# Where the modulation products of a two-layer trunk are computed: layer 1's moved into layer 0's out projection, the gate's into the attention groups

## The chip, the cores and the metric

The kernel runs on one core of a Trainium2 chip. The metric is the device time in microseconds, the median of several executions. A core has TensorE (PE in the profile; its weight loads are the row PEld), VectorE (DVE), ScalarE (ACT), GpSimd (POOL) and SyncE (SP, which here only starts DMAs). They run their own instruction streams and wait for each other on semaphores.

## The reference

Two layers over 512 tokens of width 2048, batch 1, in float32. Each layer computes, with the vector c that is the same for both layers:

```
mod = silu(c) @ w_mod[l] + b_mod[l]          # 2048 -> 3 * 2048
shift, scale, gate = split(mod, 3)
h = x * (1 + scale) + shift
p = h @ w_in[l]                              # all projections
y_nsa = nsa(...)         * silu(nz)          # 6 heads, 2 groups of 3
y_gdn = gated_delta(...) * silu(gz)          # 6 heads
y_sb  = stick_breaking(...) * silu(sz)       # 4 heads
y = concat(y_nsa, y_gdn, y_sb) @ w_out[l]    # 2048 -> 2048
x = layernorm(alpha * x + (1 + gate) * y, ln_g[l], ln_b[l])
```

`shift` and `scale` of a layer are needed at its very start, `gate` only in its out projection. `mod` depends on nothing but c and the weights, so it can be computed at any earlier time.

## The kernel before

**Matrix products.** Each float32 weight is split into a high and a low part, and a product is three TensorE passes (high x high, low x high, high x low; L439 to L441 in `column_tile`, L810 to L812 in the out projection). Weights are streamed as halves of 128 x 1024 numbers (512 KB) through a ring of four SBUF slots (`ring`, `NS = 4`). SP loads them strictly in the order of the stream (L383), each into the slot of the item four places before it, once that slot is free (`raw_free0` to `raw_free3`). GpSimd splits a half in two instructions, `w_hi` (L1170) and `w_lo` (L1172), into one of two buffers, and then frees the slot. It has to wait until TensorE has used the buffer (`split_used`). A column tile is two halves, 48 matmuls.

**Modulation products.** For layer 0, shift and scale are computed at the start of the kernel. All others go through the same ring, as items "M" between the weight items "C" and the compression weights "D": a half row block of `w_mod` (128 x 1024), which VectorE multiplies by 128 numbers of silu(c) and adds to `acc` (`add_mod`, one SCALAR_TENSOR_TENSOR on VectorE, which then frees the slot). 32 of these make one part of `mod` (2048 numbers, still to be summed over 128 partitions). Before them VectorE fills `acc` with zeros (a MEMSET of 128 x 2048) and ScalarE loads a row of `b_mod` into it (`start_sums`, L846). Behind them TensorE sums over the partitions: for shift and scale `reduce_mod` (L455, 16 matmuls with one column, two instructions each, and a copy to `modT`), for the gate four pairs of matmuls against ones (L785).

**Stages of a layer.** (1) h is built and transposed, with a small product. (2) Two attention groups (a hardware loop), each with 14 column tiles: eight first, then three heads of 11 steps, two tiles a head spread over the steps. In a head each step has scores on TensorE, a maximum on VectorE, an exponential on ScalarE, a normalisation on VectorE, transposes and the product with the values. `MOD_STEPS` says at which steps VectorE takes which Ms, ahead of its own work in that step. VectorE's last instruction of a head writes `yT`. (3) Six GDN heads. (4) Four stick-breaking heads, the first two in a loop with four column tiles each, then one with two tiles and one with one. (5) The out projection: four blocks of 512 columns, each of 8 halves (24 matmuls each) in eight banks used in turn; when a block is done, VectorE adds x, with three instructions for each of four token tiles, while TensorE is at the next block. (6) The norm, whose statistics VectorE has gathered.

**Where the Ms stand before.** Layer 0's groups take layer 1's shift (group 0) and scale (group 1): 32 Ms a group, two behind each C of the first and second head, four behind each C of the third; VectorE takes one at each of steps 0 to 7 (two in the third head). A group ends with the reduction on TensorE and a copy on VectorE. The gate's 32 Ms stand in the stick-breaking heads of each layer, eight a head. Layer 1's groups have none.

**Order.** Everything is written out by hand: the lists of items in the functions below give the order of the stream, and GpSimd's and VectorE's programs and SP's loads are derived from them. SP and GpSimd use hardware loops for the groups and lots; SP also has a loop over four slots.

Of the kernel before, what the change touches and what calls it, by code (L numbers as in the profile page):

```python
# [18 lines left out]
P = 128  # L19
# [23 lines left out]
NS = 4  # L43
# [39 lines left out]
SB_3_ITEMS = mixed(range(1), 0) + [("M", m) for m in range(8)]  # L83
GROUP_TILES = 14
LAYER_TILES = KVH * GROUP_TILES + (N_LOTS - 1) * LOT
OUT_HALVES = 2 * KT
LEVELS = (2, 4, 8, 16, 32)


def layout(has_next):  # L90

    group = len(group_items(has_next))
    at, n = {"group": SMALL_HALVES, "group_len": group}, SMALL_HALVES + KVH * group
    at["first"] = n
    n += len(FIRST_TILE)
    at["gdn"] = n
    n += GDN_H * len(GDN_ITEMS)
    at["sb"] = n
    n += (SB_H - 2) * len(SB_ITEMS)
    at["sb_2"] = n  # L100
    n += len(SB_2_ITEMS)
    at["sb_3"] = n
    n += len(SB_3_ITEMS)
    at["out"] = n
    at["end"] = n + OUT_HALVES
    return at


LAYOUTS = [layout(l < DEPTH - 1) for l in range(DEPTH)]
STREAM_AT = [sum(a["end"] - SMALL_HALVES for a in LAYOUTS[:l]) for l in range(DEPTH)]  # L110
# [54 lines left out]
def build(nc, x, positions, c, b_mod, mod0, small_cols, stream, small, lns, const, out, where, layers=DEPTH):  # L165
    x_norm = nc.dram_tensor("x_norm", (TT, P, DM), F32, kind="Internal").ap()
    ctx = ExitStack()
    with ctx:
# [55 lines left out]
        ln_gb = yT[:, 4:12, :].rearrange("p (a b) c -> p a (b c)", a=2)  # L224
        acc0 = [acc[:, :], arena[:, 16:20, :].rearrange("p a b -> p (a b)")]
# [72 lines left out]
        def spread(n, weights):  # L298
# [18 lines left out]
        MOD_STEPS = [{s: (s, s + 1) for s in range(8)}, {s: (8 + s, 9 + s) for s in range(8)},  # L317
                     {s: (16 + 2 * s, 18 + 2 * s) for s in range(8)}]
# [31 lines left out]
        turn_of_out = [(HALVES_AT[l] + LAYOUTS[l]["out"]) // NS for l in range(DEPTH)]  # L350
        sums_before = [2 + l + 2 * min(l, DEPTH - 1) for l in range(DEPTH)]
# [3 lines left out]
        def _(sp):  # L355
# [12 lines left out]
            for l in range(layers):  # L368
# [9 lines left out]
                def load(first, n):  # L378

                    with sp.Fori(0, n // NS) as n4:  # L380
                        for i in range(NS):
                            sp.wait_ge(S(f"raw_free{i}"), n4 + ((HALVES_AT[l] + first) // NS + 1))
                            sp.dma_start(ring[:, i, :], stream[bass.ds(  # L383
                                n4 * NS + (STREAM_AT[l] + first - SMALL_HALVES + i), 1)].rearrange(
                                    "a p n -> (a p) n")).then_inc(S(f"slot_in{i}"), 16)

                at = LAYOUTS[l]
                load(SMALL_HALVES, at["out"] - SMALL_HALVES)
                if l < layers - 1:

                    sp.wait_ge(S("y_ready"), after("y_ready", l * 16 + NSA_H + GDN_H))
                    sp.dma_start(sm_all[:, :], small[l + 1]).then_inc(S("small_in"), 16)
                load(at["out"], OUT_HALVES)
# [11 lines left out]
        def _(pe):  # L405
# [45 lines left out]
            def reduce_mod(sums, n):  # L451

                pe.wait_ge(S("mod_sum"), n)
                for k in range(KT):
                    last = mm(MB[:, k:k + 1], sums[:, k * P:(k + 1) * P], ones[:, 0:1], start=True, stop=True)  # L455
# [6 lines left out]
            for l in range(layers):  # L462
# [7 lines left out]
                for k in range(KT + 3):  # L470
                    if k < KT:
                        if k >= 4:

                            pe.wait_ge(S(("h_even", "h_odd")[k % 2]), l * (KT // 2) + k // 2 - 1)
                        for t in range(TT):
# [28 lines left out]
                with pe.Fori(0, KVH) as g:  # L504
# [117 lines left out]
                    if l < DEPTH - 1:  # L622

                        reduce_mod(acc, g + (sums_before[l] + 1))

# [93 lines left out]
                if l < DEPTH - 1:  # L719
                    pe.wait_ge(S("mod_copied"), 2 * l + 4)  # L720
# [68 lines left out]
                pe.wait_ge(S("mod_sum"), sums_before[l] + (3 if l < DEPTH - 1 else 1))  # L789
                gate(0, 2)  # L790
                for n in range(TT):
                    outs = (bank[2:6], ODD)[n % 2]
                    for k2 in range(KT // 2):
# [21 lines left out]
                        last.then_inc(S("split_used"), 1)  # L815


        @block.scalar
        def _(act):
# [34 lines left out]
            for l in range(layers):  # L854
# [36 lines left out]

                with act.Fori(0, KVH) as g:
# [869 lines left out]
```

## Time and profile before

| | us |
|---|---|
| median of 3 runs | 3161.83 |
| lowest and highest | 3160.68, 3165.58 |
| span of the profiled execution | 3166.5 |
| TensorE busy (86% of the span) | 2713.5 |
| VectorE busy (51%) | 1605.2 |
| GpSimd busy (47%) | 1502.6 |
| ScalarE busy (24%) | 746.3 |

The times of the runs are not split by execution, so of the profiled one only its span is given, from the first instruction to the last. A share of busy time is an average over stages that have different limits. To see what a stage is worth, the timeline shows where it begins and ends, and the views of waits and windows show who stands still in it and for whom. Matmuls overlap in the records, so the pitch from one start to the next says more than a matmul's duration.

### The profile page before, as it was taken

To read this page: it belongs to the slowest core of one execution; us is meant where nothing else is said; L and a number is where in the kernel's file an instruction comes from. 1 tells how busy PE (TensorE), PEld (TensorE's weight loads), DVE (VectorE), ACT (ScalarE), POOL (GpSimd) and SP (SyncE) were. 2 spreads that over 40 slices of the span, in tenths; PEclk is the share of its full clock that TensorE was granted. 3 is DMA by queue.
4 is the path that set the end of the run, shared out by engine and by line. 5 is a ranking of instruction groups with operands and counts; after the bars stand their busy time and mean duration, and the time that the engine had idled before them with its cause. 6 is when DMAs were issued, how large, how long until landed. Compare 5 with 4: busy or idle time off the path is not lost.

```text
span 3166.5 us, 39541 instructions
## 1 busy us (share of the span) xinstructions
PE 2713.5 (86%) x13072; PEld 2152.6 (68%) x13072; DVE 1605.2 (51%) x1975; ACT 746.3 (24%) x1332; POOL 1502.6 (47%) x692
## 2 busy tenths in 40 slices
PE   0598789878888899988987999998988888998995
PEld 0476577667777777765866777776767777775674
DVE  8615732767555553565234143146556555356535
ACT  0201100213333332333002021023323233334100
POOL 7254336433333434554762744734333334464675
PEclk9999989989999999998998999999999999998997
DMA  9433442441111111344324213211111111234431
GB/s 351 188 120 113 160 134 87 150 142 47 47 46 46 46 40 54 131 158 159 95 74 140 87 54 100 87 54 54 47 46 41 45 46 47 94 133 153 156 124 73
DMA packets 82843, 314.28 MB, mean 99 GB/s; under 512 B 9974, under 2 KB 10230, under 8 KB 76822
## 3 DMA queue, kind: packets, MB, share of 16 engines
q1 hardware_dynamic: 76608, 295.78, 28.8%
q10 hardware_dynamic: 6108, 16.83, 1.5%
q8 instruction: 78, 1.28, 0.2%
q14 instruction: 49, 0.40, 0.0%
HBM read 304.18 MB, written 8.39 MB: 99 GB/s over the span
## 4 chain that ended last, share of the span: by engine, by line
PE 44%; DVE 25%; POOLq 12%; issue 9%; ACT 4%; DMA 2%; DVEq 2%; ACTq 2%; SPq 0%
DVE arena L1216 16%; PE bank L439 8%; PE bank L441 8%; PE bank L440 8%; POOLq L1173 6%; DVE acc L1216 5%; POOLq L1171 5%; PE bank L418 3%; ACT L822 2%; PE bank L810 2%; PE bank L812 2%; PE bank L811 2%; ACT arena L822 2%; PE bank L412 2%; DVE tiny L1216 2%
## 5 line engine op out<-in xcount | busy, mean ns | idle before, releaser
L1170 POOL TENSOR_TENSOR w_hi<-ring,cst 128x1024 fp32r<-128x1024 f32 (+1 forms) x328 | 626.2, 1909 | 1575.6 <-PE bank L441 1065.4
L439 PE MATMUL bank<-h_hi,w_hi 128*128 128x512 f32 x2048 | 904.0, 441 | 46.1 <-POOLq L1173 42.9
L1172 POOL TENSOR_TENSOR w_lo<-ring,w_hi 128x1024 fp32r<-128x1024 f32 (+1 forms) x328 | 809.8, 2469 | 47.9 <-issue 0.4
L441 PE MATMUL bank<-h_hi,w_lo 128*128 128x512 f32 x2048 | 830.9, 406 | 0.0
L440 PE MATMUL bank<-h_lo,w_hi 128*128 128x512 f32 x2048 | 828.6, 405 | 0.0
L439 PEld LDWEIGHTS bank<-h_hi,w_hi 128*128 128x128 f32 x2048 | 404.5, 198 | 142.1 <-POOLq L1173 45.8
L441 PEld LDWEIGHTS bank<-h_hi,w_lo 128*128 128x128 f32 x2048 | 401.7, 196 | 92.4
L440 PEld LDWEIGHTS bank<-h_lo,w_hi 128*128 128x128 f32 x2048 | 404.9, 198 | 80.0 <-issue 13.2
L822 ACT ACTIVATE arena<-bank 128x512 f32<-128x512 f32 (+5 forms) x316 | 155.0, 490 | 982.2 <-PE bank L441 399.7
L1216 DVE SCALAR_TENSOR_TENSOR acc<-ring,cact,acc 128x1024 f32<-128x1024 f32 x128 | 216.9, 1694 | 46.0 <-DMA ring<-in_stream 29.7
L810 PE MATMUL bank<-w_hi,h_hi 128*128 128x512 f32 x512 | 202.8, 396 | 7.5 <-POOLq L1173 7.5
L822 ACT ACT_TABLE_LOAD x147 | 188.6, 1283 | 74.8 <-issue 64.8
L812 PE MATMUL bank<-w_hi,h_lo 128*128 128x512 f32 x512 | 200.6, 392 | 0.0
L811 PE MATMUL bank<-w_lo,h_hi 128*128 128x512 f32 x512 | 200.3, 391 | 0.0
L418 PEld LDWEIGHTS bank<-arena 128*128 128x128 f32 x864 | 133.9, 227 | 95.3 <-issue 87.1
L418 PE MATMUL bank<-arena 128*128 128x64 f32 x864 | 132.1, 305 | 75.0 <-DVEq L1501 49.9
L1216 DVE TENSOR_TENSOR arena<-arena,cst 128x512 f32<-128x512 f32 (+2 forms) x160 | 141.5, 885 | 38.1 <-ACT arena L822 24.0
L1216 DVE SCALAR_TENSOR_TENSOR state<-state,arena,bank 128x128 f32<-128x128 f32 x96 | 33.3, 347 | 243.8 <-PE bank L708 242.3
L1216 DVE SCALAR_TENSOR_TENSOR arena<-raw,conv_h,arena 128x512 f32<-128x512 f32 x108 | 143.6, 1329 | 9.8 <-issue 1.1
L822 ACT ACTIVATE arena<-bank,tiny 128x512 f32<-128x512 f32 (+3 forms) x132 | 75.5, 572 | 307.7 <-DVE tiny L1216 306.6
L822 ACT ACTIVATE arena<-arena 128x512 f32<-128x512 f32 (+5 forms) x186 | 95.8, 515 | 219.9 <-DVE arena L1216 187.2
L1216 DVE TENSOR_TENSOR arena<-arena,bank 128x512 f32<-128x512 f32 (+3 forms) x140 | 77.1, 551 | 131.3 <-PE bank L418 88.2
(183 smaller groups left out, 3158.0 us busy)
## 6 DMA issues: line engine op xcount, KB each, us to landing
ring<-in_stream SPq DMA_DIRECT2D x480, 512.0 KB, 3.7
yT<-in_mod SPq DMA_DIRECT2D x32, 1024.0 KB, 6.1
arena<-in_x SPq DMA_DIRECT2D x1, 4096.0 KB, 15.4
arena<-in_x ACTq DMA_DIRECT2D x4, 1024.0 KB, 10.9
x_norm<-arena ACTq DMA_DIRECT2D x4, 1024.0 KB, 7.0
arena<-x_norm ACTq DMA_DIRECT2D x4, 1024.0 KB, 9.1
out<-arena SPq DMA_DIRECT2D x4, 1024.0 KB, 3.9
raw<-in_lns ACTq DMA_DIRECT2D x8, 256.0 KB, 5.9
```

Source lines behind the costliest of these rows:

```text
L418: last = mm(narrow(dst)[:, t, :], lhs[:, t * P:(t + 1) * P], narrow(rhs)[:, t, :], start=True, stop=True)
L439: mm(PJ[b][:, :], hi, h_hi[:, k, :], start=(k == 0), stop=False)
L440: mm(PJ[b][:, :], hi, h_lo[:, k, :], start=False, stop=False)
L441: last = mm(PJ[b][:, :], lo, h_hi[:, k, :], start=False, stop=(k == KT - 1))
L810: mm(outs[t][:, :], h_hi[:, k, at], hi, start=(k == 0), stop=False)
L811: mm(outs[t][:, :], h_hi[:, k, at], lo, start=False, stop=False)
L812: last = mm(outs[t][:, :], h_lo[:, k, at], hi, start=False, stop=(k == KT - 1))
L822: made = act.activation(*args, **kw)
L1170: pool.tensor_tensor(w_hi[:, par, 0:w], ring[:, slot, 0:w], one.broadcast_to((P, w)), ALU.mult)
L1172: pool.tensor_tensor(w_lo[:, par, 0:w], ring[:, slot, 0:w], w_hi[:, par, 0:w].bitcast(F32), ALU.subtract)
L1173: pool.drain().then_inc(S("split_ready"), 1)
L1216: made = op(*args, **kw)
```

## The change

The Ms of layer 1's shift and scale leave layer 0's two attention groups and go into layer 0's out projection (64 of them), into two accumulators in `yT` (`next_acc`, blocks 4 to 11, free by then). `NEXT_MODS` gives how many Ms stand behind each half: none behind the first two or three halves of a block, three behind each of the last five (two at the very end). VectorE takes all Ms of a block before it adds x for that block. Both reductions follow TensorE's last matmul of the stage, in banks 2 and 3, and VectorE copies them before the norm. The gate's Ms leave stick-breaking and go into the groups of both layers, 16 a group: one behind each C in the first and third head, two in the second; VectorE takes them at steps 1, 4, 6 and 8. So both layers' groups are now alike, and the gate needs one fill and one row of `b_mod` ahead of the groups. The stream lies in memory as before; SP's loads, GpSimd's splits of the out projection and their addresses are written out in the new order.

```diff
+ORDER_GROUP = (mixed((0, 1), 0) + [("D", i) for i in range(8)] + mixed(range(2, 8), 0) + mixed((8, 9), 1)
+               + mixed((10, 11), 2, 4) + mixed((12, 13), 1, 12))
+ORDER_LOT, ORDER_LOT_2, ORDER_LOT_3 = (mixed(range(i), 0) for i in (LOT, 2, 1))
+NEXT_MODS = ((0, 0, 0, 3, 3, 3, 3, 3), (0, 0, 2, 3, 3, 3, 3, 3), (0, 0, 1, 3, 3, 3, 3, 3), (0, 0, 2, 3, 3, 3, 3, 2))
+def order_out(has_next):
+    items, m = [], 0
+    for n in range(TT):
+        for k2 in range(KT // 2):
+            items.append(("C", n, k2))
+            for _ in range(NEXT_MODS[n][k2] if has_next else 0):
+                items.append(("M", m))
+                m += 1
+    return items
...
+        next_acc = [yT[:, 4 * i:4 * i + 4, :].rearrange("p a b -> p (a b)") for i in (1, 2)]
...
-        MOD_STEPS = [{s: (s, s + 1) for s in range(8)}, {s: (8 + s, 9 + s) for s in range(8)},
-                     {s: (16 + 2 * s, 18 + 2 * s) for s in range(8)}]
+        MOD_STEPS = [{1: (0, 1), 4: (1, 2), 6: (2, 3), 8: (3, 4)}, {1: (4, 6), 4: (6, 8), 6: (8, 10), 8: (10, 12)},
+                     {1: (12, 13), 4: (13, 14), 6: (14, 15), 8: (15, 16)}]
...
 SP:
+                    slot, turn = (HALVES_AT[l] + p) % NS, (HALVES_AT[l] + p) // NS
+                    sp.wait_ge(S(f"raw_free{slot}"), turn + 1)
+                    sp.dma_start(ring[:, slot, :], stream[STREAM[key]]).then_inc(S(f"slot_in{slot}"), 16)
...
 TensorE, after a group (removed) and after the out projection (added):
-                    if l < DEPTH - 1:
-                        reduce_mod(acc, g + (sums_before[l] + 1))
...
+                if l < DEPTH - 1:
+                    pe.wait_ge(S("o_used"), after("o_used", l * 16 + 12))
+                    for part in range(2):
+                        reduce_mod(next_acc[part], gate_sum[l] + 1 + part, bank[2 + part])
...
 ScalarE, before its loads of x:
                 act.wait_ge(S("y_split"), l * 16 + MIX_T)
+                if l < DEPTH - 1:
+                    for part in range(2):
+                        start_sums(gate_sum[l] + 1 + part, next_acc[part][0:1, :], l + 1, part)
...
 VectorE, in the out projection:
+                if has_next:
+                    for part in range(2):
+                        fill(next_acc[part], 0.0).then_inc(S("acc_zero"), 1)
+                    dve.wait_ge(S("bmod_in"), (gate_sum[l] + 2) * 16)
                 for n in range(TT):
+                    if has_next:
+                        for m in range(sum(map(sum, NEXT_MODS[:n])), sum(map(sum, NEXT_MODS[:n + 1]))):
+                            add_mod(m, ORDER_OUT[l], l, "out", sums=next_acc[m // (2 * KT)])
+                            if m % (2 * KT) == 2 * KT - 1:
+                                sync().then_inc(S("mod_sum"), 1)
...
+                if has_next:
+                    for part in range(2):
+                        dve.wait_ge(S("mod_done"), 2 * l + 3 + part)
+                        cp(modT[:, part, :], bank[2 + part][:, 0:KT]).then_inc(S("mod_copied"), 1)
                 dve.wait_ge(S("rstd_ready"), l + 1)
```

## Rows read from the trace of the kernel before

**Rows 1.** The page: busy time; a group of instructions (busy, mean ns of one | idle before).

```profile
PE 2713.5 (86%) x13072; PEld 2152.6 (68%) x13072; DVE 1605.2 (51%) x1975; ACT 746.3 (24%) x1332; POOL 1502.6 (47%) x692
L1216 DVE SCALAR_TENSOR_TENSOR acc<-ring,cact,acc 128x1024 f32<-128x1024 f32 x128 | 216.9, 1694 | 46.0 <-DMA ring<-in_stream 29.7
```

**Rows 2.** Windows: from:to us, busy us of each engine, granted clock, DMA share, GB/s.

```profile
1350.00:1354.00 4.00, 4.00 (x10) 3.13 (x11) 3.42 (x3) 0.31 (x1) 3.85 (x2) 0.50 0.72 246
1476.00:1652.00 176.00, 171.43 (x753) 140.92 (x751) 48.70 (x54) 1.92 (x2) 132.08 (x64) 1.00 0.34 109
1862.00:1901.00 39.00, 37.66 (x197) 29.54 (x196) 19.73 (x48) 10.56 (x28) 17.43 (x9) 1.00 0.19 55
```

**Rows 3.** Timeline, start and duration in us: layer 0's out projection, first and last matmul.

```profile
1471.00 0.79 PE L810 MATMUL bank<-w_hi,h_hi 128*128 128x512 f32 x1
...
1647.04 0.39 PE L812 MATMUL bank<-w_hi,h_lo 128*128 128x512 f32 x1
```

**Rows 4.** Timeline, VectorE: starts and ends of attention heads, start of GDN, both layers.

```profile
268.72 1.28 DVE L1216 SCALAR_TENSOR_TENSOR acc<-ring,cact,acc 128x1024 f32<-128x1024 f32 x1 [0.30 <-issue]
...
314.90 0.69 DVE L1216 SCALAR_TENSOR_TENSOR yT<-bank,arena 128x512 f32 x1 [0.21 <-issue]
...
360.87 0.69 DVE L1216 SCALAR_TENSOR_TENSOR yT<-bank,arena 128x512 f32 x1 [0.21 <-issue]
...
420.30 0.69 DVE L1216 SCALAR_TENSOR_TENSOR yT<-bank,arena 128x512 f32 x1 [5.68 <-PE bank L618]
...
729.96 0.17 DVE L1216 MEMSET state<- 128x128 f32 x1 [0.29 <-issue]
...
1822.43 0.29 DVE L1216 SCALAR_TENSOR_TENSOR arena<-bank,cst 128x124 f32<-128x124 f32 x1 [0.38 <-PE bank L579]
...
1861.96 0.69 DVE L1216 SCALAR_TENSOR_TENSOR yT<-bank,arena 128x512 f32 x1 [0.22 <-issue]
...
1900.95 0.69 DVE L1216 SCALAR_TENSOR_TENSOR yT<-bank,arena 128x512 f32 x1 [0.22 <-issue]
...
1937.72 0.69 DVE L1216 SCALAR_TENSOR_TENSOR yT<-bank,arena 128x512 f32 x1 [4.53 <-PE bank L618]
...
2202.80 0.17 DVE L1216 MEMSET state<- 128x128 f32 x1 [0.30 <-issue]
```

**Rows 5.** Waits in stick-breaking, layer 0: us in total, times, longest.

```profile
PE bank L439 <- POOLq L1173: 11.0, 3, 4.6
```

**Rows 6.** Timeline: a reduction; steps 1 and 6 of a layer 1 head; a fill.

```profile
698.43 6.10 PE L455 MATMUL bank<-cst,acc 128*128 128x1 f32 x32 [1.00 <-DVEq L1400]
...
1866.80 0.29 DVE L1216 TENSOR_REDUCE tiny<-bank 128x1 f32<-128x128 f32 x1 [0.56 <-PE bank L590]
...
1883.83 0.42 DVE L1216 TENSOR_REDUCE tiny<-bank 128x1 f32<-128x256 f32 x1 [1.64 <-PE bank L590]
...
2177.02 1.76 DVE L1216 MEMSET acc<- 128x2048 f32 x1 [0.71 <-issue]
```

**Rows 7.** Timeline, VectorE and GpSimd: an M beside splits.

```profile
1404.19 2.35 POOL L1172 TENSOR_TENSOR w_lo<-ring,w_hi 128x1024 fp32r<-128x1024 f32 x1
1404.29 3.33 DVE L1216 SCALAR_TENSOR_TENSOR acc<-ring,cact,acc 128x1024 f32<-128x1024 f32 x1
...
1406.86 2.51 POOL L1170 TENSOR_TENSOR w_hi<-ring,cst 128x1024 fp32r<-128x1024 f32 x1 [0.32 <-issue]
```

**Rows 8.** Timeline, GpSimd and SP, and DMA issues (KB, us to landing): layer 0's out projection.

```profile
1573.40 2.39 POOL L1172 TENSOR_TENSOR w_lo<-ring,w_hi 128x1024 fp32r<-128x1024 f32 x1
1576.08 0.33 SPq L383 DMA_DIRECT2D ring<-in_stream  x1
1576.80 1.90 POOL L1170 TENSOR_TENSOR w_hi<-ring,cst 128x1024 fp32r<-128x1024 f32 x1 [1.01 <-PE bank L812]
...
ring<-in_stream SPq DMA_DIRECT2D x28, 512.0 KB, 3.6
```

**Rows 9.** Timeline, VectorE: the norm's first operation.

```profile
1655.99 0.16 DVE L1216 SCALAR_TENSOR_TENSOR tiny<-meanvar,tiny 128x4 f32<-128x4 f32 x1 [1.99 <-ACT tiny L822]
```

More of the change, by code:

```diff
@@ L86, with layout @@
 OUT_HALVES = 2 * KT
+ORDER_OUT = [order_out(l < DEPTH - 1) for l in range(DEPTH)]
 LEVELS = (2, 4, 8, 16, 32)
-def layout(has_next):
-    group = len(group_items(has_next))
+def layout(l):
+    group = len(ORDER_GROUP)
     at, n = {"group": SMALL_HALVES, "group_len": group}, SMALL_HALVES + KVH * group
     at["first"] = n
-    n += len(FIRST_TILE)
+    n += len(ORDER_LOT_3)
     at["gdn"] = n
-    n += GDN_H * len(GDN_ITEMS)
+    n += GDN_H * len(ORDER_LOT)
     at["sb"] = n
-    n += (SB_H - 2) * len(SB_ITEMS)
+    n += (SB_H - 2) * len(ORDER_LOT)
     at["sb_2"] = n
-    n += len(SB_2_ITEMS)
+    n += len(ORDER_LOT_2)
     at["sb_3"] = n
-    n += len(SB_3_ITEMS)
+    n += len(ORDER_LOT_3)
     at["out"] = n
-    at["end"] = n + OUT_HALVES
+    at["end"] = n + len(ORDER_OUT[l])
     return at
-LAYOUTS = [layout(l < DEPTH - 1) for l in range(DEPTH)]
-STREAM_AT = [sum(a["end"] - SMALL_HALVES for a in LAYOUTS[:l]) for l in range(DEPTH)]
+LAYOUTS = [layout(l) for l in range(DEPTH)]
+STREAM = stream_index()
 HALVES_AT = [sum(a["end"] for a in LAYOUTS[:l]) for l in range(DEPTH)]
@@ L348, in place @@
             return at % NS, at // NS + more
-        turn_of_out = [(HALVES_AT[l] + LAYOUTS[l]["out"]) // NS for l in range(DEPTH)]
-        sums_before = [2 + l + 2 * min(l, DEPTH - 1) for l in range(DEPTH)]
+        gate_sum = [2 + 3 * l + 1 for l in range(DEPTH)]
         @block.sync
@@ L376, in _ @@
                     sp.dma_start(ring[:, i, 0:4 * N_SMALL], small_cols[l, i]).then_inc(S(f"slot_in{i}"), 16)
[L378 to L393, printed above, removed]
+                for i, key in enumerate(order(l)):
+                    p = SMALL_HALVES + i
+                    if p == LAYOUTS[l]["out"] and l < layers - 1:
+                        sp.wait_ge(S("y_ready"), after("y_ready", l * 16 + NSA_H + GDN_H))
+                        sp.dma_start(sm_all[:, :], small[l + 1]).then_inc(S("small_in"), 16)
+                    slot, turn = (HALVES_AT[l] + p) % NS, (HALVES_AT[l] + p) // NS
+                    sp.wait_ge(S(f"raw_free{slot}"), turn + 1)
+                    sp.dma_start(ring[:, slot, :], stream[STREAM[key]]).then_inc(S(f"slot_in{slot}"), 16)
             for t in (1, 0, 2, 3):
@@ L1555, in split_y, with stick @@
                     tt(h_lo[:, k, :], yT[:, k, :], h_hi[:, k, :].bitcast(F32), Su).then_inc(S("y_split"), 1)
-                def stick(h, kind, items, first_k, more=0):
+                def stick(h, kind):
                     last = kind == "sb_3"
@@ L1575, in stick @@
                     for s in range(TT + 1):
-                        if s < TT:
-                            for m in (2 * s, 2 * s + 1):
-                                add_mod(m, items, l, kind, more, first_k)
-                            if last and s == TT - 1:
-                                dve.sem_inc(S("mod_sum"), 1)
                         if s < TT:
```

91 lines of the change are left out of this document (51 added, 40 removed).

## The prediction

> **What bounds the kernel now.** I read first the page's busy shares: TensorE 86%, VectorE 51%, GpSimd 47% [rows 1]. So TensorE is the base, and time is lost or won only where it waits. Then I cut the span into stages with the view of windows. In layer 0's out projection TensorE is busy 171 of 176 us at the full clock, and GpSimd, which splits each weight half into high and low parts, only 132 [rows 2]: TensorE sets the pace there, 32 halves between 1471.0 and 1647.4, 5.44 us each (first and last matmul in [rows 3]; 1.7 us of it is the gate's matmuls). In the attention groups the timeline is the view to read, because both layers run the same code there but for the modulation products (I call one such product, 128x1024, an M): layer 0 has 32 of them in each group, layer 1 none. The heads end at the writes to yT [rows 4]: layer 0's three heads take 46.2, 46.0 and 59.4 us with 8, 8 and 16 Ms, layer 1's 39.5, 39.0 and 36.8. That is the price list of an M in a head. In stick-breaking TensorE waits three times for GpSimd's splits, 11.0 us in a layer [rows 5], since Ms and weights share the four ring slots.
>
> **The change, part by part.** The sum is made against the profiled execution's own span, 3166.5 us; that is 4.7 us (0.15%) above the median of 3161.83, and the difference found is added to the median.
>
> *1. The 64 Ms of layer 1 leave layer 0's groups.* With them go two fills, two b_mod loads and two reductions on TensorE (32 instructions, 6.1 us each [rows 6]). All this together is the difference of the same stretch in both layers [rows 4]: layer 0 from 268.72 to 729.96, 461.2 us, layer 1 from 1822.43 to 2202.80, 380.4 us. Without Ms layer 0 would be like layer 1: **-81 us**. This is the surest term, a few us either way.
>
> *2. 16 gate Ms enter each of the four groups.* 4, 8 and 4 in the three heads, at steps 1, 4, 6 and 8, in pairs in the middle head. VectorE's idle time before its maximum in layer 1 is between 0.56 us (step 1) and 1.64 us (step 6) at these steps [rows 6], so an M of 1.28 us plus 0.1 to its neighbour is covered in part. By the price list: in layer 0's middle head the M of step 0 stands alone in a serial chain (2.5 us from yT to the next operation in place of 0.4: 2.1); the other seven cost 46.0 - 39.0 - 2.1 = 4.9, or 0.7 each. Doubling them, in the third head, adds 22.6 - 7.0 = 15.6 for eight, so 1.95 each, as no idle time is left. New: heads with 4 singles 2.8, the head with four pairs 4 x 0.7 + 4 x 1.95 = 10.6, a group 16 and four groups about **+62 us**. Bounds: +22 if the new places hide all but the second M of each pair (16 of 1.38 us), +108 if nothing is hidden (64 at the mean of 1694 ns [rows 1]).
>
> *3. Fill and b_mod load between groups and GDN go.* Layer 1 shows the fill alone, directly between yT and the convolutions that everything behind waits for [rows 6]: 1.76 + 0.1 us, twice, **-4 us**. The one fill now ahead of the groups stands beside TensorE's first two column tiles (16 halves would be 87 us, 4 are 22): nothing. If that cover were gone it would be 1.9 us in layer 1.
>
> *4. 32 Ms leave stick-breaking in each layer.* TensorE's three waits for splits, 4.6, 4.4 and 2.0 us, go [rows 5]. After the second the granted clock was 0.50 (the level of 1.2 GHz [rows 2]) and twelve matmuls came at 0.43 in place of 0.23 us: 2.4 more, for two heads. In the last head the pair of Ms ends at 1457.0, and the logarithm that the next operation needs was ready about 1455.6 (table load and 0.63): 1.4. Sum 17 per layer, **-34 us**; ends: -22 (the waits alone) and -50 (8 us more a layer, if the pairs of Ms in the third head, 6.2 us at 1404.29, were in the path too).
>
> *5. 64 Ms enter layer 0's out projection.* First the port. An M and a split never run together: in [rows 7] the M that begins inside w_lo (ends 1406.54) ends at 1407.62, 1.08 later, and the w_hi that begins inside the M ends 1.75 after that, at 1409.37. w_lo, 2.39 alone [rows 8], holds on in the same way for about 2.23. So the stage needs 32 x 3.98 + 64 x 1.08 + 16 VectorE sums of about 0.6 = 206 us of one thing, where TensorE needs 174. That alone is +30.
> Then the ring. Behind each of the last five halves of a column block come three Ms, so with four slots the next half falls into the slot of the half before it, and can't be fetched until that one is split. One turn, from [rows 8]: slot free to SP's issue 0.3 (1575.79 to 1576.08), landing 3.6, start 0.1, w_hi's start to w_lo's end 4.4 (1.9, 0.1 and 2.39), and one M of 1.08 between: **9.5 us** against TensorE's 5.44. There are 19 such turns. A block after the first: 8.5 for its first half, about 5.2 for each of three that are prefetched while VectorE drains the block before, 4 x 9.5: 62.3 against 43.5, three times, +56. The first block: its Ms wait for the gate (VectorE's two adds end 1491.1), two fills (3.7) and a b_mod load (2.5 at a guess, since 60 KB took 1.8), and the fifth half stands behind them in SP's queue and beside the 4 MB of x, which ScalarE now issues only after the fills: landed about 1509, split 1515, two more turns, TensorE done at 1541 in place of 1516: +25. Sum **+81 us**. Bounds: +30 (port alone), +123 (19 turns with landing 4.4 and two Ms, 11 us each, and 17 at the start). I take the turn, since every piece of it has a row.
> Here a rule is to be weighed. The Trainium skill (SBUF — State Buffer, Who interferes with whom) says that a VectorE instruction with two SBUF inputs and a GpSimd instruction that reads SBUF exclude each other for the whole instruction, so 64 x 1.28 in place of 64 x 1.08: by the page this stage would need 13 us more of the port. The row has 1.08, so I leave that out. The same page (The DMA setup-cost knee) gives 2 us and the bytes at 436 GB/s, 3.2 us for a half, an estimate; by it the turns would be 8 us cheaper in all. Here too the row, 3.6, is used.
>
> *6. The two reductions at the end of layer 0.* They stand behind the last matmul, 12.2 us (twice the 6.1), and VectorE waits for them before its two copies and the norm: about 12.8 us from the last matmul to the norm's first operation. Before it was 8.6 (1647.4 to 1655.99 [rows 9]), with ScalarE's square root in it, which is now covered: **+4 us**.
>
> *7. SP's and GpSimd's loops written out*: no instruction on the path takes longer for it; SP's issue is 0.33 us of each 5 us. Nothing; +1 to +5 if the longer program is fetched late.
>
> Sum: -81 + 62 - 4 - 34 + 81 + 4 = **+28 us**, so 3161.8 + 28 = **3190 us**.
>
> **The rivals.**
> *A. Only the port binds in the out projection (ends faster).* If halves and Ms are served so that the next half is always in a slot in time, part 5 is +30 and the whole -23: **3139 us**. For it: the loads before landed in 3.6 us, less than a half's time on TensorE. Against: the slot, which nothing but the split frees. It decides from a turn of about 8 us: 19 x 1.5 below mine is the 28 us.
> *B. The new places in the heads hide the Ms.* Part 2 is +22: -12, **3150 us**. For it: VectorE is busy 20 of 39 us in a head of layer 1 [rows 2]. Against: an M a step cost 0.7 there in steps with as much idle time.
> *C. TensorE's clock falls in the out projection.* It waits 4 us in each turn, and after such a wait the clock stood at half for 5 us [rows 2]. At 2.4 us a turn this stays inside the 9.5. If it stays at the low level (1.2 GHz), a half takes 24 x 0.43 = 10.3 us and the stage 330: 73 above the forecast, **3263 us**.
>
> **How the numbers follow.** A difference of 0.2% (6.3 us) is about what a measurement of this kernel can tell. Forecast 0.60 (3165 to 3212; 0.58 slower, 0.02 same). A 0.17 (0.13 faster, 0.04 same), B 0.13 (0.08 and 0.05), C 0.10, slower. Together faster 0.21, same 0.11, slower 0.68. The range, 3148 to 3215, takes in B, the upper part of A and the lower of C.
>
> **What would show it.** Layer 0's stretch between its groups and GDN should be about 410 us and layer 1's also (461 and 380 before); stick-breaking 191 in place of 208; TensorE's stage of the out projection 257 in place of 176, with GpSimd waiting for the ring in 19 turns of about 9.5 us, and w_lo's start to the next w_hi's 5 or more apart; the norm 13 us behind the last matmul. I am wrong if GpSimd finds its slot filled in these turns (A), if heads with four Ms take under 41 us (B), or if the granted clock of the stage is under 0.7 (C).

## The result and the profile after

| | before | changed |
|---|---|---|
| median of 4 runs, us | 3161.26 | 3188.61 |
| lowest and highest | 3159.99, 3165.58 | 3186.42, 3195.72 |
| span of the profiled execution | 3166.5 | 3187.2 |
| mean granted clock | 0.941 | 0.942 |

The ratio is 1.0089, with a 95% interval from 1.0072 to 1.0107: the changed kernel is slower by 0.9%, 27 us, where the prediction had 28 (3190 us). The spans differ by 20.7 us, less than the medians, since the profiled execution of the kernel before was the slowest of its four (3165.58).

The page of the changed kernel (busy us, share of the span; then one group: busy, mean ns of one | idle before). Against [rows 1], TensorE is busy 6.7 us longer for the same number of matmuls, so the other 14 of the 20.7 us are idle time. VectorE is busy 29.5 us longer for the same number of instructions:

```profile
PE 2720.2 (85%) x13072; PEld 2152.8 (68%) x13072; DVE 1634.7 (51%) x1975; ACT 746.2 (23%) x1332; POOL 1511.4 (47%) x692
L1256 DVE SCALAR_TENSOR_TENSOR yT<-ring,cact,yT 128x1024 f32<-128x1024 f32 x64 | 125.7, 1964 | 64.6 <-DMA ring<-in_stream 59.2
```

The timeline of the changed kernel (start, duration): the rows that answer to [rows 3, 4, 9] (heads of group 0 of layer 0, start of GDN, end of GDN and of stick-breaking, first matmul of the out projection, its two reductions, norm; then layer 1's first head and start of GDN).

```profile
268.05 0.29 DVE L1256 SCALAR_TENSOR_TENSOR arena<-bank,cst 128x124 f32<-128x124 f32 x1 [0.39 <-PE bank L625]
309.37 0.69 DVE L1256 SCALAR_TENSOR_TENSOR yT<-bank,arena 128x512 f32 x1 [0.21 <-issue]
360.45 0.69 DVE L1256 SCALAR_TENSOR_TENSOR yT<-bank,arena 128x512 f32 x1 [0.21 <-issue]
402.52 0.69 DVE L1256 SCALAR_TENSOR_TENSOR yT<-bank,arena 128x512 f32 x1 [4.51 <-PE bank L664]
...
683.74 0.17 DVE L1256 MEMSET state<- 128x128 f32 x1 [0.29 <-issue]
...
1219.48 0.75 DVE L1256 SCALAR_TENSOR_TENSOR yT<-arena,sm_all 128x512 f32<-128x512 f32 x1
...
1401.54 1.05 PE L850 MATMUL bank<-w_hi,h_hi 128*128 128x512 f32 x1
...
1406.81 0.69 DVE L1256 SCALAR_TENSOR_TENSOR yT<-bank,arena 128x512 f32<-128x512 f32 x1
...
1655.22 11.05 PE L499 MATMUL bank<-cst,yT 128*128 128x1 f32 x64
...
1662.02 0.17 DVE L1256 COPY modT<-bank 128x16 f32<-128x16 f32 x1 [0.17 <-issue]
1666.31 0.17 DVE L1256 COPY modT<-bank 128x16 f32<-128x16 f32 x1 [4.11 <-PE bank L499]
1666.57 0.16 DVE L1256 SCALAR_TENSOR_TENSOR tiny<-meanvar,tiny 128x4 f32<-128x4 f32 x1
...
1831.57 0.29 DVE L1256 SCALAR_TENSOR_TENSOR arena<-bank,cst 128x124 f32<-128x124 f32 x1 [0.39 <-PE bank L625]
...
2248.52 0.17 DVE L1256 MEMSET state<- 128x128 f32 x1 [0.29 <-issue]
```

Stick-breaking is taken from VectorE's last output of GDN to its last output of the stick-breaking heads. In the kernel before these two rows are:

```profile
1267.78 0.75 DVE L1216 SCALAR_TENSOR_TENSOR yT<-arena,sm_all 128x512 f32<-128x512 f32 x1
...
1476.02 0.69 DVE L1216 SCALAR_TENSOR_TENSOR yT<-bank,arena 128x512 f32<-128x512 f32 x1
```

Subtracting such rows gives the table of stages, in us:

| stretch | before | changed | difference | predicted |
|---|---|---|---|---|
| layer 0, first head to GDN | 461.2 | 415.7 | -45.5 | -51 |
| layer 0, stick-breaking | 208.2 | 187.3 | -20.9 | -17 |
| layer 0, out projection, first to last matmul | 176.4 | 253.8 | +77.4 | +81 |
| layer 0, last matmul to the norm's first operation | 8.6 | 11.2 | +2.6 | +4 |
| layer 1, first head to GDN | 380.4 | 417.0 | +36.6 | +30 |
| layer 1, stick-breaking | 208.5 | 187.0 | -21.5 | -17 |
| layer 1, out projection | 188.4 | 185.1 | -3.3 | 0 |

The waits of the changed kernel in 1402 to 1656 us, layer 0's out projection (engine and what it works on <- whom it waits for: us in total, times, longest), and the same for SP's queue in 1440 to 1650:

```profile
POOL w_hi L1213 <- DMA ring<-in_stream: 89.7, 19, 17.6
DVE yT L1256 <- DMA ring<-in_stream: 59.2, 24, 6.1
PE bank L850 <- POOLq L1216: 53.3, 18, 17.2
```

```profile
SPq L437 <- POOLq L1217: 137.2, 26, 6.6
SPq L437 <- DVE yT L1256: 33.0, 34, 1.7
```

These are the turns of the prediction's part 5 (its parts are called steps from here on), and the reader can go round one: TensorE waits for a split; GpSimd waits for its slot to be filled, 19 times; SP, which would fill it, waits for GpSimd to free that slot. Two turns in the timeline, GpSimd and VectorE (it answers to [rows 8]; w_hi to w_hi 8.15 and 9.59 us):

```profile
1504.76 1.90 POOL L1213 TENSOR_TENSOR w_hi<-ring,cst 128x1024 fp32r<-128x1024 f32 x1 [3.80 <-DMA ring<-in_stream]
1506.81 2.37 POOL L1215 TENSOR_TENSOR w_lo<-ring,w_hi 128x1024 fp32r<-128x1024 f32 x1
1507.15 5.87 DVE L1256 SCALAR_TENSOR_TENSOR yT<-ring,cact,yT 128x1024 f32<-128x1024 f32 x3 [2.35 <-DMA ring<-in_stream]
1512.91 1.90 POOL L1213 TENSOR_TENSOR w_hi<-ring,cst 128x1024 fp32r<-128x1024 f32 x1 [3.73 <-DMA ring<-in_stream]
1514.95 2.34 POOL L1215 TENSOR_TENSOR w_lo<-ring,w_hi 128x1024 fp32r<-128x1024 f32 x1
1515.01 6.11 DVE L1256 SCALAR_TENSOR_TENSOR yT<-ring,cact,yT 128x1024 f32<-128x1024 f32 x3 [2.00 <-DMA ring<-in_stream]
1522.50 1.90 POOL L1213 TENSOR_TENSOR w_hi<-ring,cst 128x1024 fp32r<-128x1024 f32 x1 [5.21 <-DMA ring<-in_stream]
```

The window of the stage, which answers to [rows 2] (busy us of PE, PEld, DVE, ACT, POOL; granted clock; DMA share; GB/s), and the landing of the loads in 1440 to 1650 us:

```profile
1420.00:1662.00 242.00, 188.46 (x742) 148.19 (x741) 168.49 (x120) 1.32 (x2) 133.22 (x60) 0.89 0.62 215
...
ring<-in_stream SPq DMA_DIRECT2D x83, 512.0 KB, 4.8
```

No engine is busy for more than 188 of the 242 us: what limits this stage is a chain that goes through a buffer, not a full engine.

### The profile page after: what moved, and what is told of

It is laid out like the page before. It is cut to its first block, busy times and chain, and to the rows that moved or that the text cites. A ratio compares the mean times of both kernels' runs of the same rounds, so it can differ in the third digit from the quotient of the medians.

```text
span 3187.2 us, 38168 instructions
## 1 busy us (share of the span) xinstructions
PE 2720.2 (85%) x13072; PEld 2152.8 (68%) x13072; DVE 1634.7 (51%) x1975; ACT 746.2 (23%) x1332; POOL 1511.4 (47%) x692
## 3 DMA queue, kind: packets, MB, share of 16 engines
q8 instruction: 78, 1.28, 0.2%
## 4 chain that ended last, share of the span: by engine, by line
PE 51%; DVE 25%; issue 8%; POOLq 7%; ACT 5%; ACTq 2%; DVEq 2%; DMA 1%; SPq 0%
DVE arena L1256 16%; PE bank L483 10%; PE bank L485 9%; PE bank L484 9%; POOLq L1216 4%; DVE acc L1256 4%; POOLq L1214 3%; PE bank L462 3%; ACT L867 2%; PE bank L850 2%; PE bank L852 2%; PE bank L851 2%; ACT arena L867 2%; DVE tiny L1256 2%; PE bank L456 2%
## 5 line engine op out<-in xcount | busy, mean ns | idle before, releaser
L1213 POOL TENSOR_TENSOR w_hi<-ring,cst 128x1024 fp32r<-128x1024 f32 (+1 forms) x328 | 633.8, 1932 | 1586.7 <-PE bank L485 1133.3
L483 PE MATMUL bank<-h_hi,w_hi 128*128 128x512 f32 x2048 | 897.2, 438 | 21.5 <-POOLq L1216 16.6
L850 PE MATMUL bank<-w_hi,h_hi 128*128 128x512 f32 x512 | 212.3, 415 | 59.7 <-POOLq L1216 59.5
L1256 DVE TENSOR_TENSOR arena<-arena,cst 128x512 f32<-128x512 f32 (+2 forms) x160 | 160.5, 1003 | 37.9 <-ACT arena L867 23.8
L850 PEld LDWEIGHTS bank<-w_hi,h_hi 128*128 128x128 f32 x512 | 100.4, 196 | 94.1 <-POOLq L1216 71.7
L1256 DVE SCALAR_TENSOR_TENSOR yT<-ring,cact,yT 128x1024 f32<-128x1024 f32 x64 | 125.7, 1964 | 64.6 <-DMA ring<-in_stream 59.2
```

What stands on the lines that cost most here:

```text
L483: mm(PJ[b][:, :], hi, h_hi[:, k, :], start=(k == 0), stop=False)
L850: mm(outs[t][:, :], h_hi[:, k, at], hi, start=(k == 0), stop=False)
L1213: pool.tensor_tensor(w_hi[:, par, 0:w], ring[:, slot, 0:w], one.broadcast_to((P, w)), ALU.mult)
L1256: made = op(*args, **kw)
```

## Experiments

Each ran on one chip together with the kernel before; ratios are against that kernel, with 95% intervals. The changed kernel stands at 1.0089.

### Slot or port: the out projection taken apart

**The port alone.** Nothing is loaded for the Ms, and VectorE multiplies a fixed tile.

```diff
-            for _ in range(NEXT_MODS[n][k2] if has_next else 0):
+            for _ in range(0):
...
-                            add_mod(m, ORDER_OUT[l], l, "out", sums=next_acc[m // (2 * KT)])
+                            part = next_acc[m // (2 * KT)][:, m % 2 * HALF:(m % 2 + 1) * HALF]
+                            k = m // 2 % KT
+                            stt(part, acc[:, m % 2 * HALF:(m % 2 + 1) * HALF], cact[:, 1, k:k + 1], part, M, Ad)
```

> The changed kernel, but the 64 products of the out projection are multiplied from a fixed SBUF tile and nothing is loaded into the ring for them (layer 1's shift and scale are therefore not what they should be). VectorE and its use of SBUF stay as they are, the ring slots are free for weight halves. If the slot turn sets the pace (my theory: the next half falls into the slot that the last one still holds), the stage falls from 253.8 us to what the shared port alone allows, 32 x 3.98 + 64 x 1.08 + 10 = 206 to 212 us, and the total from 3188.6 to about 3147. If the shared port between VectorE and GpSimd is the cost (rival), the stage stays at about 250 us and the total at about 3188.

Measured: 3159.27 us, ratio 1.0001 (0.9987 to 1.0014). TensorE's stage is 191.9 us, below the 206 to 212 of the slot theory; but the norm begins 43.7 us after its last matmul, in place of 11.2, and so the total misses the expected 3147 by 12 us. The timeline of VectorE in this run shows why:

```profile
1546.32 43.56 DVE L1256 SCALAR_TENSOR_TENSOR yT<-acc,cact,yT 128x1024 f32<-128x1024 f32 x16
...
1590.16 0.39 PE L852 MATMUL bank<-w_hi,h_lo 128*128 128x512 f32 x1
...
1599.80 21.68 DVE L1256 SCALAR_TENSOR_TENSOR yT<-acc,cact,yT 128x1024 f32<-128x1024 f32 x16
```

Here 16 products take 43.56 us; with no split beside them they take 21.68, 1.36 each. The windows of these two stretches (columns as above) show 15 operations of GpSimd in the first and none in the second:

```profile
1546.30:1590.00 43.70, 41.42 (x176) 32.25 (x175) 42.42 (x16) 0.00 (x0) 37.40 (x15) 1.00 0.18 51
1599.80:1621.50 21.70, 5.40 (x26) 5.31 (x25) 20.54 (x16) 0.00 (x0) 0.00 (x0) 0.50 0.00 0
```

Only the last three of the 16 products in the first stretch ran at 1.3 us, when TensorE's last half had been split. The others went in turn with GpSimd's operations, one for one:

```profile
1556.86 3.18 POOL L1215 TENSOR_TENSOR w_lo<-ring,w_hi 128x1024 fp32r<-128x1024 f32 x1
1557.87 3.25 DVE L1256 SCALAR_TENSOR_TENSOR yT<-acc,cact,yT 128x1024 f32<-128x1024 f32 x1
1560.36 2.51 POOL L1213 TENSOR_TENSOR w_hi<-ring,cst 128x1024 fp32r<-128x1024 f32 x1 [0.32 <-issue]
1561.19 2.76 DVE L1256 SCALAR_TENSOR_TENSOR yT<-acc,cact,yT 128x1024 f32<-128x1024 f32 x1
```

From w_hi to w_hi it is 6.16 us for two products and one half's two splits, 3.08 a product. TensorE's stage grows by 15.5 us, but VectorE falls behind by a whole block, and the norm waits for it.

**The slots alone.** All loads, but one SBUF input in place of two.

```diff
-                            add_mod(m, ORDER_OUT[l], l, "out", sums=next_acc[m // (2 * KT)])
+                            slot, turn = place(l, "out", ORDER_OUT[l].index(("M", m)))
+                            dve.wait_ge(S(f"slot_in{slot}"), (turn + 1) * 16)
+                            reduce(tiny[:, 31:32], ring[:, slot, :], AX, Mx).then_inc(S(f"raw_free{slot}"), 1)
```

> The changed kernel, but each of the 64 products of the out projection is replaced by a maximum over the same ring slot: one SBUF input, one column of output, about as long (layer 1's shift and scale are left out). All loads and all slots stay. If the slot turn sets the pace, only the 1.08 us that one product adds to a turn goes: 19 turns of about 8 us in place of 9.0, stage about 233 us in place of 253.8, total about 3168. If the shared port is the cost (rival), the stage comes back to 176 to 190 us and the total is about 3120.

Measured: 3179.91 us, ratio 1.0065 (1.0043 to 1.0087), stage 246.3 us. The turns are there, and their waits are those of the changed kernel (89.7 us, 19 times):

```profile
POOL w_hi L1213 <- DMA ring<-in_stream: 90.1, 19, 16.8
...
L1256 DVE TENSOR_REDUCE tiny<-ring 128x1 f32<-128x1024 f32 x64 | 78.1, 1220 | 101.7 <-DMA ring<-in_stream 97.5 <-DMA yT<-in_b_mod 1.6
```

The operation is now not stretched (1220 ns on average, against 1964 of the M), yet 70 of the 77 us remain, where 57 were expected. Over the 17 turns behind three Ms that follow the first two, w_hi starts every 8.5 us, and every 8.8 in the changed kernel: in a turn the three Ms cost 0.3 us more than the three maxima, where 1.08 was expected. VectorE takes them mostly while GpSimd waits for the load. That the port alone makes the stage longer is out.

**Neither.** No loads, and the maximum over a fixed tile, 64 times.

```diff
-                            add_mod(m, ORDER_OUT[l], l, "out", sums=next_acc[m // (2 * KT)])
+                            reduce(tiny[:, 31:32], acc[:, m % 2 * HALF:(m % 2 + 1) * HALF], AX, Mx)
```

> The changed kernel with neither loads nor port: the 64 products of the out projection become maxima over a fixed SBUF tile with one SBUF input, and nothing is loaded for them (layer 1's shift and scale are left out). VectorE is as long busy as before. If slot and port are all that the 64 products cost TensorE, its stage comes back to 176 us; since VectorE still takes 16 operations of 1.2 us before each block's sums, the last block leaves some 10 to 20 us behind the last matmul. The total is then about 3125. Rival: the unrolled program, the fills and the x loads behind them cost on their own, and the stage stays at 190 us or more.

Measured: 3106.23 us, ratio 0.9818 (0.9802 to 0.9835), stage 176.7 us, 9.3 us behind it. That is the 176.4 of before: fills, the b_mod loads, the unrolled programs and VectorE's own 78 us cost TensorE nothing. The four kernels side by side:

| | first to last matmul | from there to the norm | ratio |
|---|---|---|---|
| slots and port (the change) | 253.8 | 11.2 | 1.0089 |
| slots alone | 246.3 | 10.6 | 1.0065 |
| port alone | 191.9 | 43.7 | 1.0001 |
| neither | 176.7 | 9.3 | 0.9818 |

They don't add up, and need not: while the slot turn holds GpSimd up, the port has idle time enough for the Ms.

**Two behind a half in place of three.** The same loads and instructions in another order.

```diff
-NEXT_MODS = ((0, 0, 0, 3, 3, 3, 3, 3), (0, 0, 2, 3, 3, 3, 3, 3), (0, 0, 1, 3, 3, 3, 3, 3), (0, 0, 2, 3, 3, 3, 3, 2))
+NEXT_MODS = ((0, 0, 0, 2, 2, 2, 2, 4), (0, 2, 2, 2, 2, 2, 2, 5), (0, 2, 2, 2, 2, 2, 2, 5), (0, 2, 2, 2, 2, 2, 4, 4))
```

> The changed kernel with the same 64 products in the out projection, two behind nearly every half (NEXT_MODS (0,0,0,2,2,2,2,4), (0,2,2,2,2,2,2,5), (0,2,2,2,2,2,2,5), (0,2,2,2,2,2,4,4)) in place of three behind each of the last five. The same loads, the same instructions and the same use of SBUF; only behind two products the next half falls into a slot that is free sooner. If the slot turn sets the pace, the turns of 9.0 us go, and a half costs what the port takes, 3.98 + 2 x 1.08 = 6.1 us: the stage is 195 to 210 us in place of 253.8 and the total 3135 to 3150. If the amount of products or of loads is what costs (rival), the stage stays near 250 us and the total near 3188.

Measured: 3175.42 us, ratio 1.0046 (1.0030 to 1.0063), stage 239.2 us. The direction is the slot theory's, the size isn't: inside a block the turns are 5.4 to 7.5 us but for one of 8.6, about the 6.1 expected. But at the three borders, with four or five Ms behind the last half, they are 12.0 to 12.4, and the long turn of the first block stays (20.1 us). SP loads in order: behind a half with five Ms the fourth needs that half's own slot, so it waits for the split, and the fifth and the next half stand behind it.

**No run of Ms at the borders.** The edit is shown against the run before this one.

```diff
-NEXT_MODS = (..., (0, 2, 2, 2, 2, 2, 2, 5), (0, 2, 2, 2, 2, 2, 2, 5), (0, 2, 2, 2, 2, 2, 4, 4))
+NEXT_MODS = (..., (2, 2, 2, 2, 2, 2, 2, 2), (2, 2, 2, 2, 2, 2, 2, 2), (2, 2, 2, 2, 2, 2, 2, 6))
```

> The kernel of the run before with two behind every half of the second and third block and six at the very end (NEXT_MODS (0,0,0,2,2,2,2,4), twice (2,2,2,2,2,2,2,2), (2,2,2,2,2,2,2,6)). In that run the split of the first half of the next block began 12.0, 12.3 and 12.4 us after the last half's, where five products stand behind that half, and about 6.5 us elsewhere. If that is the same slot turn (behind three or more, a load waits for the split, and the two that follow it stand in SP's queue ahead of the next half), the two borders with two products cost about 6.5 us: stage some 12 to 15 us shorter than 239.2, minus 4 for products behind the first halves: 225 to 230 us, total about 3165. If it is VectorE that is full there (16 products beside splits and 9 us of sums a block), the borders stay at about 12 us and the stage at 237 or more.

Measured: 3179.98 us, ratio 1.0044 (1.0026 to 1.0063), stage 246.0 us. The two borders with two Ms did fall, to 5.4 and 5.8 us, as the slot theory says, but the stage didn't, and the norm begins 15.9 us behind it (10.2 in the run before). The timeline of GpSimd (w_hi), from the second half of the second block on, and the same place of the third:

```profile
1468.53 1.98 POOL L1213 TENSOR_TENSOR w_hi<-ring,cst 128x1024 fp32r<-128x1024 f32 x1 [0.32 <-issue]
1483.27 1.89 POOL L1213 TENSOR_TENSOR w_hi<-ring,cst 128x1024 fp32r<-128x1024 f32 x1 [9.95 <-DMA ring<-in_stream]
...
1528.99 2.40 POOL L1213 TENSOR_TENSOR w_hi<-ring,cst 128x1024 fp32r<-128x1024 f32 x1 [2.22 <-DMA ring<-in_stream]
1543.13 1.89 POOL L1213 TENSOR_TENSOR w_hi<-ring,cst 128x1024 fp32r<-128x1024 f32 x1 [8.96 <-DMA ring<-in_stream]
```

VectorE drains the block before (12 instructions, 10.9 us in the first of these places) while Ms already hold slots, and all that is behind them in the stream waits: 14.7, 14.1 and 16.8 us for one half. My expectation had left this out; the rival is right for the time, though by the slots that VectorE leaves filled while it drains. That is what the empty first halves of `NEXT_MODS` are for. A ring with one order has two bad places, a run of three or more and a consumer that is busy elsewhere, and neither of these two orders of 64 Ms misses both.

### What an M costs in other places

**Singles in the middle head.**

```diff
-                     {1: (4, 6), 4: (6, 8), 6: (8, 10), 8: (10, 12)}
+                     {s: (3 + s, 4 + s) for s in range(1, 9)}
```

> The changed kernel, but the middle head of each attention group takes its eight gate products one at each of the steps 1 to 8, in place of pairs at steps 1, 4, 6 and 8. If the second product of a pair is what costs (1.95 us beside 0.7 for a single one, from the heads of the kernel before), each group is 4 x 1.25 = 5 us shorter, by the measured +12.2 of that head at most 6.6: total 20 to 26 us lower, 3163 to 3169. If a product costs the same wherever it stands (rival), the total stays at 3188 and the head at 51 us.

Measured: 3182.69 us, ratio 1.0071 (1.0043 to 1.0100). The middle heads take 48.1, 48.0, 47.8 and 48.2 us. With pairs they take 49.2 to 52.5, 50.5 on average, over the 24 such heads of the changed kernel and the five others that keep the pairs. So pairs do cost more, about 2.5 us a head; but a single is not 0.7, it is (48.1 - 39.0)/8 = 1.14. The windows of the end of a middle head (columns as above), first of the kernel before, whose last M is taken at step 7, then of this one, which takes one at step 8, show where some of that comes from:

```profile
352.00:361.80 9.80, 9.26 (x57) 7.80 (x56) 5.32 (x11) 3.07 (x6) 0.07 (x1) 1.00 0.29 89
```

```profile
348.50:360.00 11.50, 8.71 (x45) 7.44 (x44) 5.50 (x10) 3.07 (x6) 3.33 (x2) 0.85 0.28 91
...
351.46 0.66 PE L656 MATMUL bank<-cst,arena 128*128 128x128 f32 x4 [2.79 <-DVE arena L1256]
...
354.25 0.63 PE L483 MATMUL bank<-h_hi,w_hi 128*128 128x512 f32 x1
...
356.06 0.39 PE L485 MATMUL bank<-h_hi,w_lo 128*128 128x512 f32 x1
```

TensorE has waited 2.79 us for the normalised probabilities, the granted clock is 0.85 in place of 1.00, and the column tile's last matmuls, which the head's end stands behind, take 0.63 us each, one every 0.43, until the clock is back (0.39, one every 0.23). The last maximum comes 37.8 us into the head (37.5 before), the head's end 10.3 us after it (8.5 before, and 8.7 in layer 1's middle head with no M). So 1.6 of the 9.1 us that the eight Ms cost come at the end of the head.

All four middle heads of this run show it. Over the runs 30 middle heads have an M or a pair at step 8. TensorE waits 2.8 to 4.4 us there, and in 29 of the 30 the granted clock of the rest of the head is 0.84 or less; in one it stays at 1.00 after a wait of 3.8. In the first and third heads an M at the same step makes TensorE wait 1.3 and 1.6 us, and the clock of the rest stays at 1.00. So the price of an M depends on the place, and on how long TensorE waits there.

The total fell by 6 us, where 20 to 26 were expected, and the 12 us of the heads are not all in it: this kernel's out projection, the same code, took 260.2 us in place of 253.8 (259.2 and 258.6 in the two runs with the gate elsewhere, below). So differences of that stage are read from one execution only where they are above 6 us.

**The gate's Ms in the GDN heads.** Eight in each of the first four heads, in both layers.

```diff
+GDN_AT = {0: (0, 2), 2: (2, 3), 3: (3, 4), 5: (4, 5), 6: (5, 7), 7: (7, 8)}
...
                     for i in range(SEQ // CHUNK):
+                        if mods and i in GDN_AT:
...
+                            for m in range(*GDN_AT[i]):
+                                add_mod(m, ORDER_GDN, l, "gdn", h * (len(ORDER_GDN) // NS), h * 4)
```

> The changed kernel, but the gate products leave the attention groups of both layers and stand in the first four GDN heads, eight a head, at recurrence steps 0, 2, 3, 5, 6 and 7, where VectorE was idle for 5.4, 1.7, 1.7, 2.2, 3.2 and 3.1 us. The groups of both layers get back the heads that layer 1 had before: 36.5 us a layer, 73 in all. If the idle time of the recurrence holds the products, a GDN stage gets 0 to 16 us longer and the total is 3116 to 3148. If a product costs its own length there as it does in the groups (rival: the recurrence is a serial chain, and its idle time is spent waiting within it), each GDN stage gets 32 x 1.2 = 38 us longer and the total is about 3190.

Measured: 3137.03 us, ratio 0.9925 (0.9899 to 0.9952). The heads of both layers are back at 39.5, 39.0 and 36.8 us, and GDN (first state to the last head's output) takes 545.8 and 546.4 us in place of 535.7 and 537.6: 32 Ms for 9 to 10 us, 0.3 each. The timeline of VectorE in it shows how they stand in the recurrence, between two updates of the state, with no idle time of VectorE above 0.48 us left:

```profile
718.46 1.28 DVE L1270 SCALAR_TENSOR_TENSOR acc<-ring,cact,acc 128x1024 f32<-128x1024 f32 x1 [0.30 <-issue]
719.91 0.35 DVE L1270 SCALAR_TENSOR_TENSOR state<-state,arena,bank 128x128 f32<-128x128 f32 x1 [0.17 <-issue]
720.74 1.29 DVE L1270 SCALAR_TENSOR_TENSOR acc<-ring,cact,acc 128x1024 f32<-128x1024 f32 x1 [0.48 <-issue]
```

**The move of layer 1's Ms alone.** The gate's stay in stick-breaking; in the last two of its heads they are multiplied by other 128 numbers of silu(c) than they should be.

```diff
-                            if s in MOD_STEPS[r]:
-                                add_mods(*MOD_STEPS[r][s])
...
+                            for m in (2 * s, 2 * s + 1):
+                                add_mod(m, items, l, kind, more, first_k)
```

> The move of layer 1's shift and scale alone: layer 0's 64 products are in its out projection as in the changed kernel, but the gate's are back in the stick-breaking heads of both layers, as before. If the parts add up, the attention groups fall by 36.5 us in each layer (both like layer 1's before), stick-breaking rises by 21 us in each, fills and b_mod loads there by about 2 each: total about 3188 - 73 + 42 + 4 = 3161. Rival: some of the change's time depends on both moves together (a queue or a slot at the border of the stages), and the total is off from that by over 8 us.

Measured: 3142.72 us, ratio 0.9934 (0.9917 to 0.9951). The sum missed by 18 us. The groups fell by the 36.5 a layer, but stick-breaking took 199.9 and 205.3 us, 13 and 18 more than in the changed kernel and not the 21 by which the kernel before stands above it, though the heads' code is that of before. Its rows, first of the kernel before and then of this one, layer 0's stick-breaking (columns as for the window above):

```profile
1267.00:1476.00 209.00, 179.63 (x701) 134.26 (x700) 132.36 (x148) 89.87 (x127) 100.81 (x45) 0.90 0.42 140
```

```profile
1176.00:1382.00 206.00, 179.86 (x733) 135.12 (x732) 128.14 (x148) 94.54 (x133) 104.48 (x46) 0.95 0.44 144
...
PE bank L489 <- POOLq L1222: 4.9, 2, 2.6
```

TensorE waits for splits 4.9 us in place of 11.0 [rows 5], and the granted clock is 0.95 in place of 0.90. Why the same items come earlier here wasn't found; the stream around them differs only in layer 0's groups and in the out projection. Read with care, the move of layer 1's Ms alone is worth -19 us, and the move of the gate's Ms into the groups, on top of it, +46: it is the second half of the change that makes it slower. The gate's move without the other was not run.

### All of it together

The gate in GDN; layer 1's shift in layer 0's groups, one at a step, reduced behind them; its scale alone in the out projection, with one M behind most halves, two at most.

```diff
+ORDER_GROUPS = [ORDER_GROUP, mixed((0, 1), 0) + [("D", i) for i in range(8)] + mixed(range(2, 14), 0)]
-NEXT_MODS = ((0, 0, 0, 3, 3, 3, 3, 3), (0, 0, 2, 3, 3, 3, 3, 3), (0, 0, 1, 3, 3, 3, 3, 3), (0, 0, 2, 3, 3, 3, 3, 2))
+NEXT_MODS = ((0, 0, 0, 1, 1, 1, 1, 1), (0, 1, 1, 1, 1, 1, 2, 2), (0, 1, 1, 1, 1, 1, 2, 2), (0, 1, 1, 1, 1, 1, 2, 2))
...
-                            if s in MOD_STEPS[r]:
+                            if has_next and s in MOD_STEPS[r]:
...
+                if has_next:
+                    sync().then_inc(S("mod_sum"), 1)
+                    dve.wait_ge(S("mod_done"), 3)
+                    cp(modT[:, 0, :], MB[:, 0:KT]).then_inc(S("mod_copied"), 1)
```

> All three lessons together: the gate's products in the first four GDN heads of both layers (measured there: 10 us a layer); layer 1's shift in layer 0's attention groups, 4, 8 and 4 a head, one at a step (about 14 us a group); layer 1's scale alone in layer 0's out projection, one product behind most halves and never three. Counted from the kernel before (3161): groups of layer 0 -81 + 28 + 3, stick-breaking -42, GDN +19, out projection +15 to +35 (32 products of 1.08 on the port beside 5.44 a half, and the start of the first block). Total 3118 to 3138 if the slot turn is gone there; if products in the out projection cost by their number (32 of 64: +39), 3145 or more.

Measured: 3101.56 us (3095.35 to 3108.04), ratio 0.9814 (0.9796 to 0.9833): 1.9% below the kernel before and 16 us below the expected range. But that range is not what its own terms give: 3161 - 81 + 28 + 3 - 42 + 19, and 15 to 35 more, is 3103 to 3123, and the measured time lies 1.5 us below that. The out projection takes 191.7 us with 32 Ms (+15.3; 64 in runs of three cost +77.4), and GpSimd waits for the ring 7 times:

```profile
POOL w_hi L1234 <- DMA ring<-in_stream: 12.3, 7, 6.9
```

Layer 0's stretch from the first head to GDN is 413.6 us, layer 1's 379.1, stick-breaking 186.7 and 187.1, GDN 537.7 and 545.9. Of the terms, GDN was too high: 19 us for both layers, where layer 0's takes 537.7 us here as in the kernel before (537.8), and 545.8 in the run with the gate alone. Why it costs nothing here is open.

## Why the prediction was right

*Steps 1 and 7* held. With no M in it, layer 0's stretch is 378.6 us (the run with the gate in GDN): 461.2 - 378.6 = 82.6, where -81 was said. The kernel with neither slots nor port shows that the unrolled programs cost the out projection nothing.

*Step 2, the Ms in the groups, was too low*: 16 a group, 19.7 measured (heads +2.2, +12.2, +5.3 in layer 1's group 0, where 2.8, 10.6 and 2.8 were said). The sum had a slip too: its own heads give 16.2 a group and 65 for four, where it has 62. The 0.7 for a single M held in the first head (0.55) and failed in the third (1.3) and in the singles run (1.14). It came from layer 0's middle head before, by taking off 2.1 for the M of step 0. Part of what it missed is the clock, which no term of the step has. In the middle head it falls behind the Ms of the head's step 8, at which the kernel before has none. In the third head it falls in the first half: these heads take 42.1 us where their granted clock is 0.96 and 40.6 in layer 1's group 1, where it is 1.00, with the same Ms. So 1.5 of the 5.3 us is the clock, and a single costs 0.9 to 1.0 there without it; why more than 0.7 isn't shown. Rival B (heads hide the Ms) is out by the groups, 19.7 us where it has 5.5. Its sign was a head with four Ms under 41 us: these take 41.3 to 42.1, and the one of 40.6.

*Step 3*, the fills between the groups and GDN, was not measured by itself; it is inside the two rows of the table.

*Step 4*: stick-breaking gained 4 us more than said in each layer (-20.9 and -21.5 against -17), inside the bounds. The changed kernel has no wait of TensorE for splits there, and its granted clock is 0.94 against 0.90.

*Step 5, the out projection*: +77.4 against +81, with exactly the 19 waits foreseen. In the three other runs with the same out projection it is +82 to +84, so the term is right within what one execution can tell. The mechanism is shown by removing either half of it: slots alone 246.3 us, port alone 191.9. The parts of the term are less exact. The first block takes 74.8 us where 70 was said, with one wait of 17.6 us in which w_hi to w_hi is 22.1. The other three take 60.2, 60.9 and 57.9 where 62.3 was said, since the turn is 8.8 us and not 9.5. What was too large in the turn is the M's 1.08: GpSimd's wait from w_lo's end to the next w_hi is 3.7 to 5.2 us in the turns shown, where issue and landing alone were put at 4.0.

The port was priced right where it binds. In the run with the port alone, two Ms and one half's splits take 6.16 us together; the prediction's 3.98 + 2 x 1.08 is 6.14. But the bound of +30 assumed that all 64 Ms stand beside splits while TensorE works. It was +15.5 on TensorE and +35 more behind it, since VectorE was late and took the last 16 after the last matmul. The rule of the Trainium skill weighed there (SBUF — State Buffer, Who interferes with whom: the two engines exclude each other) has the direction of this run, 3.08 us a product beside splits against 1.36 alone. It does not have the size: if each waited for the other's whole instruction, two of 1.28 and splits of 1.90 and 2.39 would take 6.85 us, where 6.16 is measured, so the row was rightly preferred. Rival A was out already by the waits.

*Step 6* was +2.6 (4 said): the two reductions took 11.05 us together, not twice 6.1.

Rival C is out: the granted clock of the stage is 0.89.

The errors of steps 2 (+15), 4 (-8), 5 (-4) and layer 1's out projection (-3.3, not foreseen) cancel. That the total came out within 1 us is luck. What was right is the direction of every part, and the mechanism and size of the largest, step 5.

## What to carry to other kernels

With a ring that is filled in order, count for each item which item had its slot before, and who frees that one: a second kind of item in runs of (slots - 1) or more makes every load wait for the work that should hide it, and the stage then runs at issue + landing + work, whatever the busy shares say. Before side work is moved to where an engine looks idle, price it there by a run with it and one without; here one M cost 1.2 us in the out projection and the attention heads, 0.4 to 0.65 in stick-breaking, and 0.3 or less in the recurrence of GDN, which neither kernel used. Give the slack in a serial recurrence the side work first, and take two suspected causes away one at a time and both together, since costs that share the same idle time don't add.

## What the runs showed of the hardware

- VectorE products with two SBUF inputs (128x1024) went one for one with GpSimd's splits, one every 3.08 us, and one every 1.36 without them; a maximum over as much data with one SBUF input took 1.22 us on average in the same stage. GpSimd's w_lo took 3.18 us beside such products, and 2.37 on average with the maximum.
- The median landing of a 512 KB load rose from 3.6 us (109 GB/s) to 4.8 us (215 GB/s, three or four issued one behind another).
- After a wait of 2.79 us in an attention head, TensorE's matmuls of a column tile came every 0.43 us for some 3 us, in place of 0.23. After waits of 1.3 and 1.6 us in other heads they didn't.
- TensorE's granted clock was 0.89 in a stage where it waited 18 times for a split, 53.3 us in all, and 1.00 in the same stage before [rows 2].
